# Key selection shared between VectorE and ScalarE, the sample's loads in another order, and the conv branch's swish ahead of the prompt's attention

## The reference

```python
h = x + 0.5 * g1 * swiglu(modulate(x, g_ffn1, s1, sc1), w1_gate, w1_up, w1_down)
n = modulate(h, g_mix, s2, sc2)
u, q, k, v, qi, ki, wi, g_c, g_a = split_in(n, w_in, ...)     # u = a_lin * sigmoid(a_gate)
# conv branch: causal depthwise conv (31 taps), LayerNorm over 512 channels, silu, w_conv_out
y = depthwise_conv(concat(prefix, u), w_dw) + b_dw
conv_out = silu(layernorm(y, ln_g, ln_b)) @ w_conv_out
# sparse attention
s = sum_h wi[t,h] * relu(qi[t,h] . ki[s]);  keep the 256 largest admissible keys of each row
att = softmax-attention over the kept keys (8 heads of 64) @ w_attn_o
h = h + g2 * ((sigmoid(g_c) * conv_out + sigmoid(g_a) * att) @ w_out)
h = h + 0.5 * g3 * swiglu(modulate(h, g_ffn2, s3, sc3), w2_gate, w2_up, w2_down)
y = rmsnorm(h, g_final)
```

## Time and profile before

| | |
|---|---|
| median of 3 runs | 2652.9 us (2650.93 to 2660.53) |
| the profiled execution: own time | 2649.56 us |
| its span | 2647.8 us |
| granted clock over the span | 0.97 of full speed |
| TensorE busy | 2481.5 us (94%) |
| VectorE busy | 1436.0 us (54%) |
| ScalarE busy | 621.0 us (23%) |
| GpSimd busy | 1459.0 us (55%) |

### The profile page before, as it was taken

How to read it: one execution, slowest core, us unless ns; L and a number is a source line. 1 busy time by engine, 2 the same in 40 slices (tenths; PEclk the granted TensorE clock), 3 DMA queues, 4 the chain that set the end, 5 groups by cost and what they waited for, 6 DMA issues and landing times.

```text
span 2647.8 us, 44576 instructions
## 1 busy us (share of the span) xinstructions
PE 2481.5 (94%) x16038; PEld 2305.4 (87%) x16038; DVE 1436.0 (54%) x2646; ACT 621.0 (23%) x1149; POOL 1459.0 (55%) x1234
## 2 busy tenths in 40 slices
PE   5999999999998888899999769999899999999997
PEld 3899999999997856699998436789799999999997
DVE  5543334444446637899998745462564444444444
ACT  3311011111113323312334357310511111111113
POOL 1276666666665235546998020124057777777774
PEclk8999999999999979999999779999999999999999
DMA  8422222222221532321224500234011111111112
GB/s 287 120 69 75 72 71 64 78 79 79 79 72 61 143 79 77 87 84 47 89 97 166 192 1 1 89 107 146 0 33 48 48 48 54 50 53 48 48 48 82
DMA packets 242984, 209.98 MB, mean 79 GB/s; under 512 B 14671, under 2 KB 207299, under 8 KB 241977
## 3 DMA queue, kind: packets, MB, share of 16 engines
q1 hardware_dynamic: 232700, 181.70, 22.9%
q10 hardware_dynamic: 10181, 26.90, 3.1%
HBM read 173.03 MB, written 28.94 MB: 76 GB/s over the span
## 4 chain that ended last, share of the span: by engine, by line
PE 83%; DVE 7%; issue 4%; ACT 3%; DMA 1%; SPq 1%; POOL 1%; ACTq 0%; DVEq 0%; POOLq 0%
PE main L763 11%; PE main L764 10%; PE main L765 10%; PE main L295 7%; PE main L296 7%; PE main L297 7%; PE main L864 5%; PE main L866 5%; PE main L865 5%; DVE pick L1698 2%; PE main L2103 1%; PE main L2120 1%; PE aux L2131 1%; PE aux L763 1%; PE aux L764 1%
## 5 line engine op out<-in xcount | busy, mean ns | idle before, releaser
L684 POOL TENSOR_TENSOR blo<-raw,bhi 128x512 fp32r<-128x512 f32 x424 | 553.5, 1305 | 34.0
L682 POOL CAST bhi<-raw 128x512 fp32r<-128x512 f32 x424 | 264.5, 624 | 545.5 <-PE main L866 312.0
L763 PE MATMUL main<-nhi,bhi 128*128 128x352 f32 x1312 | 429.2, 327 | 18.0 <-issue 10.9
L764 PE MATMUL main<-nlo,bhi 128*128 128x352 f32 x1312 | 423.2, 323 | 0.0
L765 PE MATMUL main<-nhi,blo 128*128 128x352 f32 x1312 | 423.0, 322 | 0.0
L295 PE MATMUL main<-nhi,whi 128*128 128x352 f32 x1032 | 339.7, 329 | 1.0 <-DVE pick_s L1686 0.5
L297 PE MATMUL main<-nhi,wlo 128*128 128x352 f32 x1032 | 333.4, 323 | 0.0
L296 PE MATMUL main<-nlo,whi 128*128 128x352 f32 x1032 | 333.3, 323 | 0.0
L1100 DVE SCALAR_TENSOR_TENSOR h<-main,ada,h 128x352 f32<-128x352 f32 (+1 forms) x448 | 251.9, 569 | 84.5 <-PE main L866 84.5
L864 PE MATMUL main<-hid_hi,bhi 128*128 128x352 f32 x896 | 292.2, 326 | 4.8 <-DVE h L1100 2.9
L866 PE MATMUL main<-hid_hi,blo 128*128 128x352 f32 x896 | 288.0, 321 | 0.0
(11 more groups left out here) (371 smaller groups left out, 4974.9 us busy)
## 6 DMA issues: line engine op xcount, KB each, us to landing
raw<-in_w_gate SPq DMA_DIRECT2D x44, 512.0 KB, 4.2
raw<-in_w_up SPq DMA_DIRECT2D x44, 512.0 KB, 3.9
ada_part<-in_w_ada SPq DMA_DIRECT2D x44, 512.0 KB, 4.9
raw<-in_w_down SPq DMA_DIRECT2D x44, 512.0 KB, 3.9
raw<-in_w_in SPq DMA_DIRECT2D x40, 512.0 KB, 3.8
ada_raw<-in_w_ada SPq DMA_DIRECT2D x7, 2048.0 KB, 12.4
gate_d<-zraw ACTq DMA_DIRECT2D x16, 528.0 KB, 2.7
gates<-gate_d SPq DMA_DIRECT2D x16, 528.0 KB, 4.7
```

The source lines that it names most:

```text
L682: pool.tensor_copy(bhi[:, slot], src).then_inc(sg.block_hi.sem, 1)
L684: pool.tensor_tensor(blo[:, slot], src, bhi[:, slot].bitcast(F32), ALU.subtract)\
L763: pe.matmul(out, bhi[:, slot, w], hi(c), start=start and c == 0, stop=False, skip_group_check=True)
L764: pe.matmul(out, bhi[:, slot, w], lo(c), start=False, stop=False, skip_group_check=True)
```

## The change

Three parts. **(1)** In 30 of the 31 rounds of `threshold` the widest block (1024 keys) is no longer counted by VectorE. VectorE makes a copy of its scores with the lowest bit set (`odd`), sends the negated trial as `bound_s`, and ScalarE adds up the signs of `odd` less the bound and turns the sum into `over` (`sign_count`). These counts stand in ScalarE's order behind fixed evacuations of the z stage (`sign_counts_at`). **(2)** SP loads `vraw` in two halves first, then key pages 4 and 5, `ka`, key pages 6 and 7, the conv state, and `qa` only after the values are turned. **(3)** LayerNorm scaling and swish of all three chunks go ahead of the prompt's attention, and `ln_squares(2)` ahead of the sample's value products; GpSimd waits once for all three chunks.

```diff
+        SIGN_BLOCKS = (0,)
+        NSIGN = len(SIGN_BLOCKS)
+        odd = place("odd", [P, NSIGN, SEQ], F32, HB + 2 * 4 * TOK)
+        signs = place("signs", [P, 2, SEQ], BF16, UB + 29696)
...
+        def sign_count(act, n):
+
+            sel_bound.wait(act, 1 + 2 * NSIGN + n)
+            for k, i in enumerate(SIGN_BLOCKS):
+                act.activation(signs[:, k, 0:width(i)], odd[:, k, 0:width(i)], ACT.Sign, bias=bound_s[:, k:k + 1],
+                               accum_out=sum_s[:, k:k + 1]).then_inc(sel_sign.sem, 1)
+            for k, i in enumerate(SIGN_BLOCKS):
+                sel_sign.wait(act, NSIGN * (n + 1))
+                act.activation(over[:, i:i + 1], sum_s[:, k:k + 1], ACT.Identity, scale=0.5, bias=mid_s[:, k:k + 1])\
+                    .then_inc(sel_over.sem, 1)
+
+        def sign_counts_at(L, t):
+            e = 3 * (L - Z_V - 1) + t
+            return [n for n in range(SIGN_BIT - 1) if int(2.0 + 1.3 * n) == e]
...
+                for n in sign_counts_at(L, t):
+                    sign_count(act, n)
                 for i in PRODUCTS_AT.get(L, [])[t:t + 1]:
...
+            for k, i in enumerate(SIGN_BLOCKS):
+                dve.tensor_scalar(odd[:, k, 0:width(i)].bitcast(U32), scores_of(i).bitcast(U32), 1, None,
+                                  ALU.bitwise_or).then_inc(sel_bound.sem, 1)
...
-                for i in range(NSEL):
-                    count((n + 1) * NSEL + i, i, trial[:, i:i + 1])
+                blocks = [i for i in range(NSEL) if bit == 0 or i not in SIGN_BLOCKS]
+                for i in blocks:
+                    count(made, i, trial[:, i:i + 1])
+                    made += 1
...
+                if bit:
+                    sel_over.wait(dve, NSIGN * (n + 1))
...
+                if bit > 1:
+                    dve.wait_ge(sel_step, 3 * n + 2)
+                    for k, i in enumerate(SIGN_BLOCKS):
+                        last = dve.tensor_scalar(bound_s[:, k:k + 1], trial[:, i:i + 1], -1.0, None, ALU.mult)
+                    last.then_inc(sel_bound.sem, 1)
...
-            sp.dma_start(ka[:, :, :], k_d).then_inc(k_in, 16)
-            sp.dma_start(qa[:, :, :], q_d).then_inc(k_in, 16)
+            sp.dma_start(vraw[:, 0:2, :], v_d[:, 0:2, :]).then_inc(v_in, 16)
+            sp.wait_ge(cv_sum, NPROD)
+            sp.dma_start(vraw[:, 2:4, :], v_d[:, 2:4, :]).then_inc(v_in, 16)
             for b in range(4, 6):
                 sp.wait_ge(kp_t, 2 * (b - 3))
                 keys_of(b)
-            sp.wait_ge(cv_sum, NPROD)
-            sp.dma_start(vraw[:, :, :], v_d).then_inc(v_in, 16)
-            sp.dma_start(out[9][0][:, 0:HIST - SNEW, :], L0["state_conv"][:, SNEW:HIST, :]).then_inc(u_out, 16)
-
+            sp.dma_start(ka[:, :, :], k_d).then_inc(k_in, 16)
             for b in range(6, NSEQ):
                 sp.wait_ge(kp_t, 2 * (b - 3))
                 keys_of(b)
+            sp.dma_start(out[9][0][:, 0:HIST - SNEW, :], L0["state_conv"][:, SNEW:HIST, :]).then_inc(u_out, 16)
             sp.wait_ge(kv_t, 9)
+            sp.dma_start(qa[:, :, :], q_d).then_inc(v_in, 16)
             for b in range(4):
                 values_of(b)
...
+            ln_squares(2)
             for half in range(2):
-                if half:
-                    ln_squares(2)
                 pe.wait_ge(vp_in[half], 32 * 4)
...
+            ln_swish(0)
+            ln_swish(1)
             act.wait_ge(so_t, 1)
             act.activation(o_hi[:, :, SEQ:TOK], ...)
+            ln_swish(2)
...
             ln_scale(0)
             for half in range(2):
+                if half:
+                    ln_scale(1)
                 dve.wait_ge(so_mm, 4 * half + 4)
...
+            ln_scale(2)
             dve.wait_ge(so_e, 1)
```

More of the change, by code:

```diff
@@ L1173, in build @@
         over, miss, sgn, taken = (place(n, [P, 6], F32) for n in ("over", "miss", "sgn", "taken"))
+        SIGN_BLOCKS = (0,)
+        NSIGN = len(SIGN_BLOCKS)
+        odd = place("odd", [P, NSIGN, SEQ], F32, HB + 2 * 4 * TOK)
+        signs = place("signs", [P, 2, SEQ], BF16, UB + 29696)
+        bound_s, mid_s, sum_s = (place(n, [P, NSIGN], F32) for n in ("bound_s", "mid_s", "sum_s"))
         trial, found = aux[:, 0, 0:6], aux[:, 1, 0:6]
@@ L1550, in threshold @@
             dve.memset(trial[:, :], 2.0).then_inc(idx_set, 1)
+            dve.memset(bound_s[:, :], -2.0).then_inc(sel_bound.sem, 1)
             dve.wait_ge(idx_set, 9 + 3)
@@ L1569, in threshold @@
                     dve.wait_ge(sel_step, 3 * n - 1)
-                for i in range(NSEL):
-                    count((n + 1) * NSEL + i, i, trial[:, i:i + 1])
-                    if n and i == 0:
+                blocks = [i for i in range(NSEL) if bit == 0 or i not in SIGN_BLOCKS]
+                for i in blocks:
+                    count(made, i, trial[:, i:i + 1])
+                    made += 1
+                    if n and i == blocks[0]:
                         dve.tensor_tensor(found[:, :].bitcast(U32), found[:, :].bitcast(U32), taken[:, :].bitcast(U32),
                                           ALU.bitwise_or).then_inc(sel_step, 1)
-                dve.wait_ge(sel_count, (n + 2) * NSEL)
+                dve.wait_ge(sel_count, made)
+                if bit:
+                    sel_over.wait(dve, NSIGN * (n + 1))
                 if n:
@@ L1584, in threshold @@
                         .then_inc(sel_step, 1)
+                if bit > 1:
+                    dve.wait_ge(sel_step, 3 * n + 2)
+                    for k, i in enumerate(SIGN_BLOCKS):
+                        last = dve.tensor_scalar(bound_s[:, k:k + 1], trial[:, i:i + 1], -1.0, None, ALU.mult)
+                    last.then_inc(sel_bound.sem, 1)
             dve.tensor_tensor(taken[:, :].bitcast(U32), taken[:, :].bitcast(U32), found[:, :].bitcast(U32),
                               ALU.bitwise_or).then_inc(sel_step, 1)
-        SEL_STEPS = 3 * SIGN_BIT - 1
+            dve.wait_ge(sel_step, SEL_STEPS - 1)
+            dve.scalar_tensor_tensor(taken[:, :], taken[:, :], SMALLEST, taken[:, :], ALU.is_ge, ALU.mult)\
+                .then_inc(sel_step, 1)
+        SMALLEST = 2.0 ** -126
+        SEL_STEPS = 3 * SIGN_BIT
         def keep_largest(dve):
@@ L2029, in m2_pe @@
             pe.wait_ge(u_e, 2)
-            pe.wait_ge(v_in, 16)
+            pe.wait_ge(v_in, 32)
             for t in range(9):
@@ L2034, in m2_pe @@
                 sample_logits(b)
-            pe.wait_ge(k_in, 32)
+            pe.wait_ge(k_in, 16)
             for t in range(9):
@@ L2091, in m2_pe @@
             pe.wait_ge(so_e, 2)
-            pe.wait_ge(k_in, 32)
+            pe.wait_ge(v_in, 48)
             def logits(u):
@@ L2266, in m2_act, with ln_swish @@
                     .then_inc(ln_sem["sd"], 1)
+            def ln_swish(t):
+                act.wait_ge(ln_sem["ml"], t + 1)
+                for c in range(4):
+                    last = act.activation(conv_y[:, c, tcs(t)], conv_y[:, c, tcs(t)], ACT.Silu,
+                                          scale=par[:, ROW_LNG + c:ROW_LNG + c + 1],
+                                          bias=par[:, ROW_LNB + c:ROW_LNB + c + 1])
+                last.then_inc(ln_sem["af"], 1)
+            ln_swish(0)
+            ln_swish(1)
             act.wait_ge(so_t, 1)
@@ L2283, in turned @@
                         .then_inc(pt_e, 1)
-            def ln_swish(t):
-                act.wait_ge(ln_sem["ml"], t + 1)
-                for c in range(4):
-                    last = act.activation(conv_y[:, c, tcs(t)], conv_y[:, c, tcs(t)], ACT.Silu,
-                                          scale=par[:, ROW_LNG + c:ROW_LNG + c + 1],
-                                          bias=par[:, ROW_LNB + c:ROW_LNB + c + 1])
-                last.then_inc(ln_sem["af"], 1)
             for n in range(NQ + 8):
@@ L2295, in m2_act @@
                     turned(n - 2)
-                if n == LN_SWISH:
-                    for t in range(NTC):
-                        ln_swish(t)
                 if n % H == 5 and n > H:
```

9 lines of the change are left out of this document (5 added, 4 removed).

## The result

| | before | after |
|---|---|---|
| median of 8 runs | 2653.2 us (2650.9 to 2664.3) | 2639.8 us (2638.1 to 2650.8) |
| profiled execution, own time | 2649.56 us | 2641.70 us |
| its span | 2647.8 us | 2639.9 us |
| VectorE busy | 1436.0 us | 1401.2 us |
| ScalarE busy | 621.0 us | 662.7 us |

The ratio of the times is 0.995, 95% interval 0.9933 to 0.9967: 13 us faster (9 to 18), at the edge of what such a measurement can tell. All intervals are of fast runs; one slow run, 3518.7 us among the twelve of swish_late, is left out. The forecast was 2641, in a range of 2626 to 2651.

The account below looks back on a forecast made before the run. TensorE bounds the kernel, meeting the SP queue at the value products. Loads 3.0 us later, half clock 3.0 later, scaling and swish 17.8 earlier sum to -11.8 us, from 2652.9 to 2641 us for the median, range 2626 to 2651.

Parts of the forecast that it names:

- part 1 on TensorE's path: Z stage: sign counts bring VectorE out about 30 us earlier, but change nothing on TensorE's path.
- SP's order: SP's loads before the value pages: three separate loads holding page reads 13.8 us against 10.8, so 3.0 us later.
- products and fold at half clock: Value products and fold before the first logits: half clock after TensorE's wait of some 15 us, 3.0 us later.
- waits in the attention, less the first exp's delay: Attention: scaling's waits go, 5.6 us, and the swish's, 8.7 us, less 0.5 us delay of the first exp.
- clock in the attention: Attention: work at about half clock behind waits comes back, 2.5 us after the swish, 1.5 us behind two shorter waits.
- first mixing product: End of the attention, 1686 us before: some 12 us earlier, the forecast's sum of -11.8 us.
- What bounds: Start of the attention: TensorE and the SP queue arrive together, so TensorE's 13.8 us count only if SP gives time back.
- The block around the swish: Attention: 1.30 us from table load to first swish, no drain; the skill's 2.66 us switch would make it 2.8 us longer.
- the loads hold the reads longer: Rival on SP's page reads: pages end some 13 us later instead of 3, total 2651 us; chance 0.15.
- the reads are hardly held: Rival on SP's page reads: SP ends up to 10.8 us earlier, total 2627 us; chance 0.13.
- The stall of the z stage: Rival in the z stage: VectorE-ScalarE handshake rounds outrun the PSUM cover, +18 us, total 2671 us; chance 0.05.
- the waits of the attention only change their owner: Rival in the attention: other engines still pace narrow blocks, only the swish pays, about -3 us, 2650 us; chance 0.08.

Follow-up runs that it names:

- swish_late: Changed kernel with all three swish chunks back in the attention (step 16), scaling left ahead of it; ratio 0.9985 (0.9965 to 1.0004) to the kernel before.
- loads_only: Kernel before with only the second part, SP's new load order and TensorE's matching waits; ratio 1.0008 (0.9991 to 1.0025) to the kernel before.
- no_signs: Changed kernel without its first part, VectorE counting all six blocks again; ratio 0.9949 (0.993 to 0.9968) to the kernel before.
- pages_kept: Changed kernel with page numbers kept in SP's registers from the z stage's indexer reads; 2628.3 us median, ratio 0.9904 to the kernel before.
- signs_only: Kernel before with only the first part, ScalarE counting the widest block by signs; ratio 0.9997 (0.9983 to 1.0012) to the kernel before.
- norm_only: Kernel before with only the third part, scaling, swish and third chunk's squares ahead of the attention; ratio 0.9949 (0.993 to 0.9968).

## Why the prediction was right, and where it was not

| step of the sum | forecast | in the two traces |
|---|---|---|
| part 1 on TensorE's path | 0 | 0 |
| SP's order | +3.0 | 0.0 |
| products and fold at half clock | +3.0 | +3.1 |
| waits in the attention, less the first exp's delay | -13.8 | -13.2 |
| clock in the attention | -4.0 | +1.4 |
| start of the sample part | 0 | +1.6 |
| first mixing product | -11.8 | -7.2 |

**What bounds.** Right. TensorE and the SP queue do meet at the value products, and the 13.8 us for `vraw` came back as 12.2 us for a page. loads_only, no_signs and pages_kept show it from three sides.

**Part 1.** Right at every place I named: TensorE 170 of 170 us at full clock while the rounds run, round 5.02 us (5.0), conv groups' end 1459.4 (1460), lateness 3.1 us (2 to 4), no effect (signs_only). `odd` took 0.69 us, where I took 1.35 between bounds of 0.17 and 2.7.

**Part 2.** The mechanism was right, the size was off. I let each of three separate loads hold back the page reads by 4.6 us, as `vraw` had. Counted in the same way, less 2.74 for a step and the issue: behind the second half of `vraw` the page comes after 6.05 us, so 2.5 (with 0.8 for the issues) are held; behind `ka` after 6.81, 3.6; behind the conv state and `qa` 5.45 and then 4.33 us, some 3.9 together. That is 10.0 instead of 13.8, and with 10.8 before it SP's length doesn't change. The reads themselves say the same: a page takes two of them, of 1.25 and 0.45 us by the median, and behind the second half of `vraw` they took 3.72 and 1.05, behind `ka` 2.86 and 2.89. The bytes loaded are the same in both orders; that the hold goes by them and not by the number of loads fits this, but was not tried. The nearest row was one load, and one row was too few. Against it I had set a rule of the Trainium skill (DMA: Bandwidth & Descriptors, Queues, rings and completion order: a DMA engine serves its queues in turn, packet by packet), by which I took the reads to be hardly held. They are held, up to 3.7 us for a read of 1.25 (the spread of these reads in the changed kernel); whether a read goes through those queues at all, no run shows.

```profile
L1925 SPq TENSOR_LOAD <-in_page_table_ptr x24: 1003/1252/3718, 1443.9 to 1519.6; - x24
```

**Part 3.** TensorE's idle time in the attention fell from 156.47 - 129.58 = 26.9 us to 144.70 - 131.02 = 13.7 us, 13.2 where I had 13.8. These are the windows of TensorE over the attention, of the kernel before and of the changed one:

```profile
1530.54:1687.01 156.47, 129.58 (x1089) 0.89 0.03 9
```

```profile
1535.08:1679.78 144.70, 131.02 (x1088) 0.90 0.03 9
```

The idle time is a firm figure: it was 26.1 to 26.9 us in the four kernels with the old attention and 13.7 to 14.4 in the nine with the new one.

The block around the swish was what the rows said, not the 2.66 us per switch that the Trainium skill states (ScalarE: Activation LUTs, What ACT_TABLE_LOAD costs). In the changed kernel too a first swish follows 1.30 us after its load's start, and the load starts 0.01 us after the end of the instruction before it:

```profile
1509.38 0.56 ACT L2306 ACTIVATE rstd_c<-main,cst 128x352 f32<-128x352 f32 x1 [1.81 <-PE main L2095]
1509.95 1.28 ACT L2313 ACT_TABLE_LOAD   x1
1511.25 2.39 ACT L2313 ACTIVATE conv_y<-conv_y,par 128x352 f32<-128x352 f32 x4
```

**The clock in the attention is the step that failed.** I counted 2.5 + 1.5 us for work that ran at half clock because it followed a wait. Busy time rose by 1.4 us instead. The 1.5 us were put down to the wrong thing: the clock doesn't fall behind the two shorter waits. It stands at its lower level over the whole head of the attention, with these waits and without them, and it did so for 29 us here. Windows of TensorE in the changed kernel:

```profile
1540.00:1544.00 4.00, 4.00 (x20) 0.50 0.01 2
...
1560.00:1564.00 4.00, 4.00 (x19) 0.50 0.02 4
1564.00:1568.00 4.00, 3.70 (x26) 0.98 0.00 0
```

In the profiled execution of the kernel before it had ended sooner than it mostly does, as its windows show beside those of signs_only, whose attention is the same code and starts at the same time:

```profile
1548.00:1552.00 4.00, 4.00 (x16) 0.50 0.00 0
1552.00:1556.00 4.00, 3.38 (x20) 0.67 0.00 0
1556.00:1560.00 4.00, 3.70 (x31) 1.00 0.01 2
```

```profile
1552.00:1556.00 4.00, 3.38 (x18) 0.50 0.00 0
1556.00:1560.00 4.00, 4.00 (x20) 0.50 0.00 0
1560.00:1564.00 4.00, 3.35 (x20) 0.82 0.00 0
```

Three kernels with the attention of before took 158.7, 159.3 and 159.6 us for it, the profiled execution of before 156.5; the nine with the new one lie between 143.4 and 144.7, swish_late aside. So the one trace from which I worked flattered the kernel before by some 3 us, and that of the changed kernel began its sample part 1.6 us late (in twelve of the fourteen kernels that start lies anywhere from 1437.3 to 1440.7, loads_only's at 1440.7 with nothing changed ahead of it). With both taken out, 7.9 + 3 + 1.6 = 12.5 us, and the 13.3 of the times is met. So the clock term, too, has to be read in more than one trace. TensorE was busy for 132.6, 132.7 and 133.3 us in those three attentions, for 131.0 in the changed kernel's and for 129.0 to 131.0 in all nine:

```profile
1530.37:1689.68 159.31, 132.69 (x1088) 0.87 0.03 9
```

This row is of signs_only (stretch, length, TensorE's busy time, clock). Against these three the clock gave back 1.6 to 2.3 us in the changed kernel, not 4. What there is of it goes with the swish: in all five kernels that have it in the attention the clock falls to 0.50 a second time, in its wait, for some 10 to 14 us, and in the nine others it isn't. The attention as a whole became 14 to 15 us shorter by this reading, where I had forecast 17.8 (11.8 by the two profiled executions alone). The forecast of the time was good because two errors cancelled, the 3.0 us for SP's order that did not come and the 3 us or so too many in the attention, not because each term was right: that part is luck.

**The rivals.** That the loads hold the reads longer and that the reads are hardly held both fell: SP's length stayed the same. The stall of the z stage fell with signs_only. That the waits of the attention only change their owner fell with norm_only.

## What to carry to other kernels

When two engines reach a place together, price a saving on one by the other: here two parts of three only moved TensorE's wait from `vraw` to the value pages, and the third part alone had the whole gain. A stretch of small loads whose addresses are read from DRAM at each step is bound by those reads (2.7 us per page here, against 0.9 once the numbers were kept in registers: 14.24 us for 16); look for a place where the same numbers have been read before, since that was worth another 12 us on top of the change, while reading them early in the kernel before gave nothing. And a duration or a clock level that is read from one profiled execution should be looked for in a second place before it carries a term of a few us.

## What the runs showed of the hardware that I had not expected

- TensorE's clock stood at its lower level (1.2 GHz) through the first 22 to 33 us of the prompt's attention in every kernel (22 us in swish_late, 33 in loads_only; 24 to 29 in the nine with the new attention; in two kernels it fell within about 1 us of the first logits and not ahead of them), though TensorE was busy for 80 to 100% of several of these stretches (4.00 of 4.00 us in 1540 to 1544, clock 0.50), and also after 24 products back to back. In the changed kernel it rose 4 us behind the start of the first block of 384 keys (1560.09). What makes it rise was not tried, and stays open.
- In two of fourteen kernels the sample part started 7 to 11 us later than in the others (1446.7 and 1449.1). In both the extra time lies in the first 100 us of the span, where the clock was 0.81 and 0.78 on average, against 0.91 in before, and TensorE's records number 400 and 391 against 451; nothing of the change runs there. This spread, of about 10 us between executions, is as large as the effect under study, which is why the traces, compared from the first sample product on, told more than the medians.
- A product of 128x128 by 512 columns in f32 took 0.87 us at full clock (20.87 us for 24, two records each). The LayerNorm sums of 352 columns took 0.61 (4.90 us for 16 records, eight products), so the price goes with the columns here.
